# Stick-breaking attention: the order of work in the first and the last pair of heads

## What is computed

```python
def _sb_attend(qs, qpos, kvs, kpos):
    (q,) = qs
    k, v = kvs
    z = jnp.einsum('bqhd,bkhd->bhqk', q, k).astype(jnp.float32) * (HEAD_DIM ** -0.5)
    mask = kpos[None, :] < qpos[:, None]
    log_keep = jnp.where(mask, jax.nn.log_sigmoid(-z), 0.0)
    later = lax.cumsum(log_keep, axis=3, reverse=True) - log_keep
    a = jnp.where(mask, jnp.exp(jax.nn.log_sigmoid(z) + later), 0.0)
    return jnp.einsum('bhqk,bkhd->bqhd', a.astype(v.dtype), v)

def sb_mixer(h, w_qkv, w_o):
    B, L, _ = h.shape
    qkv = (h @ w_qkv).reshape(B, L, 3, N_HEADS, HEAD_DIM)
    q, k, v = qkv[:, :, 0], qkv[:, :, 1], qkv[:, :, 2]
    o = sweep_queries(_sb_attend, (q,), (k, v))
    return o.reshape(B, L, N_HEADS * HEAD_DIM) @ w_o
```

## Time and profile before

| | us |
|---|---|
| median of 3 runs | 1033.28 |
| lowest and highest | 1031.31, 1033.63 |
| profiled execution, time | 1030.09 |
| profiled execution, span of the core | 1028.3 |
| PE busy in the span | 987.6 (96%) |
| DVE busy | 825.8 (80%) |
| ACT busy | 565.1 (55%) |

### The profile page before, as it was taken

The page is one execution under the profiler, slowest core; times in us unless marked ns, Lnnn a source line. Parts: engine busy times, 40 slices in busy tenths (PEclk is TensorE's granted clock), DMA queues, the critical chain, the costliest instruction groups (busy, mean ns, idle before and its releaser), DMA issues.

```text
span 1028.3 us, 19503 instructions
## 1 busy us (share of the span) xinstructions
PE 987.6 (96%) x7946; PEld 956.1 (93%) x7946; DVE 825.8 (80%) x1388; ACT 565.1 (55%) x1062; POOL 111.4 (11%) x130
## 2 busy tenths in 40 slices
PE   6999999999999999999999999999999999999996
PEld 6999999999888879999999998898999999999995
DVE  7888898887798876899979878888998668766543
ACT  5755455345666655556555535665545466655532
POOL 3100000211000004002203310122000210000001
PEclk9999999999999999999999999999999999999999
DMA  8555557665423324799858824232345435555441
GB/s 238 222 199 208 206 203 264 239 235 206 144 103 123 104 103 140 275 333 316 287 201 309 306 78 163 102 136 93 131 165 180 172 141 206 206 192 177 165 164 41
DMA packets 33881, 192.19 MB, mean 187 GB/s; under 512 B 4976, under 2 KB 6272, under 8 KB 15104
## 3 DMA queue, kind: packets, MB, share of 16 engines
q1 hardware_dynamic: 23440, 157.36, 42.6%
q10 hardware_dynamic: 6912, 25.17, 7.2%
q0 software_dynamic: 3440, 8.42, 2.6%
HBM read 187.78 MB, written 3.15 MB: 186 GB/s over the span
## 4 chain that ended last, share of the span: by engine, by line
PE 71%; DVE 19%; ACT 5%; issue 3%; DMA 2%; POOL 0%; DVEq 0%; ACTq 0%; POOLq 0%
PE ps L93 70%; DVE wl L70 6%; ACT wh L67 2%; PE ps L96 1%; DVE a L70 1%; DMA raw<-w 1%; DVE b L70 1%; ACT s L67 1%; DVE s L84 1%; DVE natl L70 1%; DVE s L77 1%; DMA fz<-fz 1%; DVE x L73 0%; DVE x L70 0%; DVE yl L70 0%
## 5 line engine op out<-in xcount | busy, mean ns | idle before, releaser
L70 DVE TENSOR_TENSOR wl<-raw,wh 128x1024 fp32r<-128x1024 f32 x283 | 342.7, 1225 | 25.4 <-ACT wh L67 25.0
L67 ACT ACTIVATE wh<-raw 128x1024 fp32r<-128x1024 f32 x286 | 296.2, 1049 | 28.9 <-DMA raw<-w 12.4
L93 PE MATMUL ps<-xh,wh 128*128 128x256 f32 (+1 forms) x992 | 279.0, 281 | 3.9 <-DVE wl L70 2.7
L93 PE MATMUL ps<-xh,wl 128*128 128x256 f32 (+1 forms) x992 | 277.0, 279 | 0.0
L93 PE MATMUL ps<-xl,wh 128*128 128x256 f32 x992 | 276.9, 279 | 0.0
L93 PE MATMUL ps<-xt,wh 128*128 128x272 f32 (+1 forms) x1120 | 219.8, 291 | 3.2 <-DVE ps L70 1.5
L93 PEld LDWEIGHTS ps<-xh,wh 128*128 128x128 f32 x992 | 186.9, 188 | 5.0 <-issue 2.4
L93 PEld LDWEIGHTS ps<-xh,wl 128*128 128x128 f32 x992 | 187.5, 189 | 0.2
L93 PEld LDWEIGHTS ps<-xl,wh 128*128 128x128 f32 x992 | 187.4, 189 | 0.0
L93 PEld LDWEIGHTS ps<-xt,wh 128*128 128x128 f32 x1120 | 178.8, 190 | 6.3 <-issue 3.5
L93 PE MATMUL ps<-xt,wl 128*128 128x272 f32 (+1 forms) x560 | 160.8, 287 | 0.0
(11 more groups left out here) (351 smaller groups left out, 1609.4 us busy)
## 6 DMA issues: line engine op xcount, KB each, us to landing
raw<-w SPq DMA_DIRECT2D x141, 1024.0 KB, 4.9
ada<-ada ACTq DMA_DIRECT2D x42, 512.0 KB, 4.3
cb<-ada ACTq DMA_DIRECT2D x6, 512.0 KB, 5.0
raw<-w SPq DMA_DIRECT2D x4, 512.0 KB, 6.5
spare<-w SPq DMA_DIRECT2D x2, 1024.0 KB, 9.1
spectra<-ev POOLq DMA_DIRECT2D x8, 256.0 KB, 3.6
skew<-rpb POOLq DMA_DIRECT2D x8, 192.0 KB, 3.6
x<-x POOLq DMA_DIRECT2D x2, 544.0 KB, 9.5
```

The source lines that it names most:

```text
L67: return Issued(self.e and self.e.activation(out, src, func, **kw))
L70: return Issued(self.e and self.e.tensor_tensor(out, a, b, op))
L93: return Issued(self.e and self.e.matmul(out, stat, mov, start=start, stop=stop))
```

## The change

Four things are moved; no instruction is added or taken away.

- DVE, pair 0: the low part of the half that v of pair 2 will use (`self.rests(V, W.spent(("v", 0)))`) stood ahead of the pair's first steps, and stands behind the six steps of head 0.
- ACT, pair 0: `softs(0, 1)` stood behind `qh` of pair 2 and one cast of weights, and stands ahead of them.
- PE, pair 7: of `sbo(2, 0, 5)`, which stood ahead of `out_pe` of pair 6, tiles 0 to 2 stand behind it, and tiles 3 and 4 behind the scores of head 1, together with tile 5.
- DVE, pair 7: the modulation sum stood ahead of the steps of head 1, and stands behind `ttl(7)`. The call with place 1, which did nothing, is gone.

```diff
--- before.py
+++ after.py
@@ -1392,11 +1392,13 @@
             elif p == 6:
                 sbo(0, 0, 5)
             else:
-                sbo(0, 5, 6), sbo(1, 5, 6), sbo(2, 0, 5)
+                sbo(0, 5, 6), sbo(1, 5, 6)
             if p:
                 self.out_pe(P, p - 1)
             else:
                 self.vt_pe(P, 0)
+            if p == 7:
+                sbo(2, 0, 3)
             self.scores_pe(P, p, 1, 0)
             self.scores_pe(P, p, 1, 1)
             if p < 6:
@@ -1404,7 +1406,7 @@
             elif p == 6:
                 sbo(1, 0, 3)
             else:
-                sbo(2, 5, 6)
+                sbo(2, 3, 6)
             self.turns_pe(P, p, 0, 0)
             self.turns_pe(P, p, 0, 1)
             if p < 6:
@@ -1549,9 +1551,12 @@
             if p:
                 oh(p - 1)
             if p < 6:
+                if p == 0:
+                    softs(0, 1)
                 qh(p + 2, 0)
                 self.casts(A, W.spent(("q", p + 2)))
-            softs(p, 1)
+            if p:
+                softs(p, 1)
             if p < 6:
                 qh(p + 2, 1)
             weights(p, 1, 0)
@@ -1667,11 +1672,12 @@
             qf(p), kvf("k", p), ql(p, 0), ql(p, 1), kl(p)
             self.rests(V, W.spent(("k", p)))
         kvf("v", 0)
-        self.rests(V, W.spent(("v", 0)))
         for p in range(8):
             if p == 7:
                 vl(7)
             soft(p, 0, 0), soft(p, 0, 1), later(p, 0, 0), later(p, 0, 1), kept(p, 0, 0), kept(p, 0, 1)
+            if p == 0:
+                self.rests(V, W.spent(("v", 0)))
             if p < 7:
                 vl(p)
             if p < 6:
@@ -1683,7 +1689,8 @@
                 ql(p + 2, 0)
             elif p == 7:
                 self.rests(V, W.spent(("v", 7)))
-            self.ada_dve(V, ("sb", p), 0)
+            if p < 7:
+                self.ada_dve(V, ("sb", p), 0)
             soft(p, 1, 0), later(p, 1, 0), soft(p, 1, 1), kept(p, 1, 0), later(p, 1, 1), kept(p, 1, 1)
             if p < 6:
                 ql(p + 2, 1)
@@ -1696,7 +1703,8 @@
                 kvf("v", p + 1)
             atl(p, 1)
             ttl(p)
-            self.ada_dve(V, ("sb", p), 1)
+            if p == 7:
+                self.ada_dve(V, ("sb", p), 0)
             if p < 7:
                 self.rests(V, W.spent(("v", p + 1)), True)
         ol(7)
```

## The result

| | before | after |
|---|---|---|
| median of 4 runs, us | 1032.54 | 1026.96 |
| lowest and highest | 1031.31, 1033.63 | 1025.57, 1027.46 |
| ratio, 95% interval | | 0.9947 [0.9930, 0.9964] |
| profiled execution, time | 1030.09 | 1026.83 |
| profiled execution, span | 1028.3 | 1025.0 |

The change makes the kernel faster by 0.53%, 5.6 us between the medians; 4.6 was forecast. The predicted 1028.7 was counted from a median of 1033.28, which with a fourth run became 1032.54; counted from that, the forecast is 1027.9.

What follows compares the result with a forecast made beforehand. TensorE, busy 96% of the span, was taken as the bound, so only its waits and lower-clock time could be won. Pair 0's 2.6 plus pair 7's 2.0 made 4.6 us: 1033.28 - 4.6 = 1028.7, range 1026.4 to 1031.4.

Steps and rivals of the forecast that it cites:

- Pair 0, 2.6 us: Pair 0's DVE and ACT moves: scores start without waiting, head 1's turn at 270.9 instead of 273.49, 2.6 us won.
- The lower bound: Pair 0 term: 0.1 us if the scores stayed at 267.28 and only ACT's order changed.
- Pair 7, 2.0 us: Pair 7's PE and DVE moves: head 1's turn at 380.5 instead of 382.45, 2.0 us won.
- The wait left: Pair 7: PE still waits 0.6 us before head 1's turn, where 1.73 was.
- The halves alone: Pair 7: 0.85 us won without the sum's move, 0.7 without PE's order; neither would do alone.
- Nothing in between gave the gain back: Pairs 1 to 6: what pair 0 wins is carried to pair 7, as long as DVE and ACT follow PE.
- The fall of the clock: After PE's 2.02 us wait in pair 0: lower clock makes 3.5 us of 1.75 us work; cost little there.
- The rival with the further fall: Pair 7: a fall behind the wait at 382.45 goes too, 4.6 + 1.75 = 6.35, so 1026.9 us; chance 0.14.
- the sum gave 1025.5: Whole kernel: 2.6 + 2.0 = 4.6 us off the profiled execution's 1030.09 gives 1025.5.
- One place only: Either pair 0 or pair 7 pays: 1031.3 with 2.0 left, 1030.7 with 2.6 left; chance 0.12.
- nothing moves: Another wait ends last at both places, gain under 2 us, 1032.5 us; chance 0.11.
- Slower by falls: Remaining or moved waits bring additional falls at 1.75 us each; four cost 7.0, giving 1035.7 us; chance 0.05.

Runs made afterwards that it cites:

- softs_only: Kernel before with only ACT's softs(0, 1) in pair 0 moved ahead of qh and the cast; 1032.21 us, ratio 0.9999.
- pair0_only: Kernel before with only the two moves in pair 0 (low part on DVE, softs on ACT), none in pair 7; 1029.24 us, ratio 0.9971.
- low_part_only: Kernel before with only DVE's low part in pair 0 moved behind head 0's steps; 1031.17 us, ratio 0.9999.
- sbo_only: Kernel before with only PE's tiles of sbo(2) in pair 7 moved; 1030.55 us, ratio 0.9985.
- before_again: The unchanged kernel before, executed and traced once more; 1031.66 us (one run).
- before_third: The unchanged kernel before, executed and traced a third time; 1030.93 us (one run).
- the second comparison: The changed kernel unaltered, timed again beside the kernel before: 1027.19 against 1031.97 us, ratio 0.9957.
- sum_only: Kernel before with only the modulation sum of pair 7 moved behind ttl on DVE; 1030.05 us, ratio 0.9977.
- ql_wl_late: Changed kernel plus, on DVE, pair 0's ql of pair 2 and pair 7's wl put behind head 1's steps; 1026.06 us, ratio 0.9941 to before.
- cast_late: ql_wl_late plus, on ACT in pair 0, both halves of qh together and the cast behind head 1's exponential; 1025.18 us, ratio 0.9931 to before.
- pair7_only: Kernel before with only the two moves in pair 7 (sbo(2) tiles on PE, modulation sum on DVE); 1029.42 us, ratio 0.9973.
- after_again: The changed kernel unaltered, timed and traced once more; 1027.19 us, ratio 0.9957 to before.

## Why the prediction came out as it did

**Pair 0, 2.6 us: right, by its own steps.** Measured 2.53 against the same trace (2.36 against the two executions of before without a fall). By distances: head 0's steps 2.16 earlier (2.17 forecast), scores 2.09 earlier and without a wait (265.2 instead of 267.28, 2.08), head 1's steps 26.04 - 23.71 = 2.33 earlier (2.4), DVE idle for `qh` 1.14 (1.1), the new wait of PE 0.96 (0.9). The lower bound, 0.1 with ACT's order alone, met 0.02 in softs_only, by luck: the steps came 0.32 earlier there, and a fall hid it.

**Pair 7, 2.0 us: right.** Measured 1.99. The scores came 132.04 - 128.14 = 3.90 earlier, of which 1.37 belong to pair 7 (1.4 forecast). The wait left was 0.44 where 0.6 was forecast. The halves alone gave 0.92 (forecast 0.85) and 0.73 (0.7). The sum's 1.14 us were covered by DVE's idle time, which fell by 1.15.

**Nothing in between gave the gain back.** pair0_only shows 2.53 at the turn of pair 0 and 2.48 seven pairs on.

**The fall of the clock: the mechanism was right, the price of 1.75 too high.** An uncovered fall cost 1.54, 1.48, 1.51 and 1.49 us (pair0_only, low_part_only, softs_only, sbo_only). The prediction counted the whole stretch at the lower clock as work at half pace; the end-to-end distances give some 0.25 less. The covered fall in pair 0 cost 0.17.

**The rival with the further fall was a part of the truth.** The prediction gave it 0.14, with nothing in its trace for it. Its argument, that the timed runs lay one or two falls above the profiled one, doesn't hold: the profiled execution had three falls in its span, before_again and before_third one each, and these two were longer all the same, by a first feed-forward layer of 185.08 us instead of 183.16. Nor does the rule that the prediction quotes say that a wait of this length brings a fall; it says that the moment of a change differs from run to run. But the timed runs of the changed kernel do have about 1.2 falls fewer. Falls behind pair 7's long wait happened in 3 of 7 executions that had this wait. If they come as often in the kernel before, that is worth 3/7 x 1.5 = 0.6 us on average, on top of 4.5; not 1.75. None followed the shortened wait in the 7 executions that have it. With it the sum would be 4.5 + 0.6 = 5.1, between the measured 4.8 and 5.6. That this is what the timed runs gained isn't shown: their mean clock doesn't say where a fall was, and the three traced executions of the kernel before had none there.

**The step that was missing** is a term on the stages behind the attention. The prediction took them as unchanged, and in the traces of the changed kernel the last layer was 1.3 us longer. So the profiled execution came to 1026.83, where the sum gave 1025.5: +0.53 up to the norm's row, -4.52 in the attention, 0 in the first layer, -0.57 in the middle, +1.31 in the last layer, 3.25 less in all. The mean span of three traced executions went from 1029.1 to 1025.4, by 3.7; the medians of the timed runs differ by 4.8 and 5.6. The 1.1 to 1.9 us between these are within the noise: the intervals of the two ratios are 3.7 to 7.2 and 2.7 to 6.2 us, so neither shuts out 3.7, the first only just. The falls may be 0.6 of it. That the forecast of 4.6 lies so near the 4.8 of the second comparison is in part luck: it left out two things of opposite sign, the falls and the last layer.

**The rivals that fell.** "One place only" and "nothing moves" would have shown in the distances; both places paid in full in three of three traces. "Slower by falls" needed falls behind the new short waits; there was none.

## What to carry to other kernels

Read a wait together with what stands next in the queue of the engine that ends it: here the order of two engines had to change at once, and either alone gave next to nothing (softs_only) or moved the wait to a place where it cost a fall of the clock (low_part_only). A wait of TensorE of around 2 us can cost its own length and 1.5 us more, and a trace without a fall behind it doesn't rule that out: in pair 0 the same wait of the same kernel had one in one trace and none in two. Behind the waits of 1.24 us and less in the attention there was no fall in any trace. A fall costs time only where PE's work right behind it is what the rest waits for. Check a gain stage by stage with distances from a common row: the difference between two spans mixes in stages that have nothing to do with the change.

## What the runs showed of the hardware

**The pace of a stream of matmuls at full clock has more than one value.** In the last layer PE is busy all the time, and the clock is 1.00. Windows of before:

```profile
870.00:930.00 60.00, 60.00 (x501) 60.00 (x501) 43.41 (x67) 36.10 (x88) 0.00 (x0) 1.00 0.57 197
975.00:1005.00 30.00, 30.00 (x267) 30.00 (x266) 14.87 (x16) 13.79 (x20) 2.97 (x4) 1.00 0.39 141
```

and of after:

```profile
870.00:930.00 60.00, 60.00 (x505) 60.00 (x505) 43.20 (x66) 36.31 (x88) 0.00 (x0) 1.00 0.56 195
975.00:1005.00 30.00, 30.00 (x257) 30.00 (x256) 14.79 (x15) 13.70 (x19) 2.96 (x4) 1.00 0.33 122
```

Before does 60/501 = 0.120 us a matmul in the first stretch and 30/267 = 0.112 in the second; after 0.119 and 0.117. It gains a little first and loses more in the end. The end points in PE's timeline of before:

```profile
838.69 0.59 PE L93 MATMUL ps<-sq,ones 128*128 128x256 f32 x2
...
1018.56 0.70 PE L93 MATMUL ps<-sq,ones 128*128 128x256 f32 x2 [0.59 <-ACT sq L67]
```

and of after:

```profile
834.13 0.59 PE L93 MATMUL ps<-sq,ones 128*128 128x256 f32 x2
...
1015.31 0.70 PE L93 MATMUL ps<-sq,ones 128*128 128x256 f32 x2 [0.59 <-ACT sq L67]
```

179.87 against 181.18 us. All 14 traces have one of these two lengths (within 0.03): 179.86 or 179.87 in the kernel before (3 traces), low_part_only, sbo_only, sum_only, ql_wl_late and cast_late, and 181.15 to 181.18 in the changed kernel (3 traces), pair0_only, pair7_only and softs_only. Where a kernel was traced three times it had the same one each time, so it seems to go with the program, though none of these programs differs there in PE's order. It is not the chip: ql_wl_late and after_again ran on the same chip, and so did sum_only and softs_only, with one length each. In the first layer the length changes between executions of one and the same kernel (183.16 and 185.08 in before, 183.16 to 183.18 and 185.08 in after), with 183.48 in ql_wl_late and softs_only, and 188.06 in the profiled execution of pair7_only, which took 1034.39 and is the longest of its twelve. What sets the pace wasn't tried: no experiment changed it on purpose. It is a matter of 1 to 5 us in a kernel of 1030, as much as the change itself, and a part of why the spans and the timed runs don't give the 4.52 us of the attention.

**The clock falls behind the same wait in some executions and not in others.** Behind the 2.02 us it fell in 4 of 7 executions, among them one of three of the kernel before. Behind the 1.59 to 1.73 us of pair 7 it fell in 3 of 7, but no kernel was seen both ways there. A fall cost about 1.5 us where nothing covered it, and 0.17 where PE would have waited anyway.

**Falls lie outside the attention too.** Windows of before:

```profile
23.00:27.00 4.00, 4.00 (x22) 4.00 (x21) 2.67 (x9) 3.15 (x6) 3.29 (x2) 0.57 0.02 6
651.00:655.00 4.00, 4.00 (x21) 4.00 (x22) 3.74 (x7) 2.21 (x6) 2.16 (x2) 0.57 0.26 47
```

The first kind follows a wait of PE of about 1.5 us at 22 us and is there in 8 of the 14 traces. The second lies between 638 and 656 us, behind a wait of 1.6 to 1.7 us, and is there in 10 of them. Neither shows in the times: the norm's row at 245 us lies at 245.66 us on average with the first fall and at 245.64 without, and the middle stage took 251.1 to 252.2 us with the second and 251.5 to 251.8 without. So the number of falls doesn't give their price. What covered these wasn't looked into.
